# VectorE's low half of a weight one fetch after ScalarE's high half, in the attention part of block 1

## The reference, cut to what matters

```
for i in range(2):
    h = rms_norm(x, ln_attn_g[i])
    dq, dk, dv, mq, mk, mv = split(h @ w_in[i])        # six sections of 512 columns
    dq, dk, mq, mk = rms_norm(each head of them)
    y_diff = diff_attention(dq, dk, dv, ...)           # 4 heads, two score maps each
    y_moba = moba_attention(mq, mk, mv, ...)           # 8 heads; 256 tokens are one block
    x = x + concat(y_diff, y_moba) @ w_out[i]
    x = x + conv_ffn(rms_norm(x, ln_ffn_g[i]), ...)    # not touched
```

## Time and profile before

| | us |
|---|---|
| median of three timed runs (2045.48 to 2047.96) | 2046.79 |
| the profiled execution, its own time | 2051.6 |
| its span in the trace | 2049.8 |
| mean granted TensorE clock, share of full speed | 0.996 |

### The profile page before, as it was taken

How to read it: one execution, slowest core, us unless ns; L and a number is a source line. 1 busy time by engine, 2 the same in 40 slices (tenths; PEclk the granted TensorE clock), 3 DMA queues, 4 the chain that set the end, 5 groups by cost and what they waited for, 6 DMA issues and landing times.

```text
span 2049.8 us, 33452 instructions
## 1 busy us (share of the span) xinstructions
PE 2009.4 (98%) x13114; PEld 1738.3 (85%) x13114; DVE 1330.0 (65%) x2339; ACT 955.7 (47%) x1574; POOL 159.3 (8%) x169
## 2 busy tenths in 40 slices
PE   9999999999999999999999999999999999999998
PEld 7779998878999888888888788888878899888997
DVE  6767667767877337476445555868566686575665
ACT  4655555565555434353432453233246454445444
POOL 2001000000110100000200001111110000100100
PEclk9999999999999999999999999999999999999999
DMA  8446665535555322222222104534234244441554
GB/s 248 148 142 245 228 225 196 181 108 175 186 176 191 137 93 81 75 83 83 72 93 93 52 31 157 193 116 161 92 129 154 93 135 155 134 154 57 193 172 134
DMA packets 79706, 285.54 MB, mean 139 GB/s; under 512 B 8976, under 2 KB 9644, under 8 KB 79552
## 3 DMA queue, kind: packets, MB, share of 16 engines
q1 hardware_dynamic: 71136, 256.93, 37.7%
q10 hardware_dynamic: 6416, 19.51, 2.7%
q0 software_dynamic: 2000, 6.97, 1.3%
HBM read 277.55 MB, written 5.83 MB: 138 GB/s over the span
## 4 chain that ended last, share of the span: by engine, by line
PE 81%; DVE 10%; ACT 6%; issue 2%; DMA 1%; POOL 0%; ACTq 0%; DVEq 0%; SPq 0%
PE pb L1124 16%; PE pb L1126 15%; PE pb L1125 15%; PE pb L1137 6%; PE pb L1139 6%; PE pb L1138 6%; DVE SPL L2222 3%; ACT SPH L1637 3%; PE pb L1143 3%; PE pb L1302 2%; PE pb L1496 2%; PE pb L1303 2%; PE pb L1304 2%; PE pb L1477 2%; PE pb L1391 1%
## 5 line engine op out<-in xcount | busy, mean ns | idle before, releaser
L2222 DVE TENSOR_TENSOR SPL<-RAW,SPH 128x1024 fp32r<-128x1024 f32 x460 | 558.9, 1232 | 367.2 <-ACT SPH L1637 343.4
L1637 ACT ACTIVATE SPH<-RAW 128x1024 fp32r<-128x1024 f32 x462 | 477.4, 1052 | 208.4 <-PE pb L1126 111.3
L1124 PE MATMUL pb<-HTH,SPH 128*128 128x256 f32 (+1 forms) x1304 | 447.0, 343 | 8.4 <-POOL HTL L2881 3.1
L1126 PE MATMUL pb<-HTH,SPL 128*128 128x256 f32 (+1 forms) x1304 | 437.9, 336 | 0.0
L1125 PE MATMUL pb<-HTL,SPH 128*128 128x256 f32 (+1 forms) x1304 | 437.5, 335 | 0.0
L1124 PEld LDWEIGHTS pb<-HTH,SPH 128*128 128x128 f32 x1304 | 247.8, 190 | 36.8 <-ACT HTH L1686 3.2
L1126 PEld LDWEIGHTS pb<-HTH,SPL 128*128 128x128 f32 x1304 | 247.8, 190 | 26.1
L1125 PEld LDWEIGHTS pb<-HTL,SPH 128*128 128x128 f32 x1304 | 248.0, 190 | 24.8
L1137 PE MATMUL pb<-SPH,HTH 128*128 128x512 f32 x640 | 254.6, 398 | 2.1 <-DVE SPL L2222 1.4
L1139 PE MATMUL pb<-SPL,HTH 128*128 128x512 f32 x640 | 249.9, 390 | 0.0
L1138 PE MATMUL pb<-SPH,HTL 128*128 128x512 f32 x640 | 249.8, 390 | 0.0
(11 more groups left out here) (297 smaller groups left out, 2853.2 us busy)
## 6 DMA issues: line engine op xcount, KB each, us to landing
RAW<-in_w_up SPq DMA_DIRECT2D x88, 512.0 KB, 4.5
RAW<-in_wa SPq DMA_DIRECT2D x64, 512.0 KB, 3.5
RAW<-in_w_in SPq DMA_DIRECT2D x48, 512.0 KB, 4.7
RAW<-in_wmg SPq DMA_DIRECT2D x48, 512.0 KB, 3.5
RAW<-in_wbr SPq DMA_DIRECT2D x48, 512.0 KB, 3.5
RAW<-in_w_down SPq DMA_DIRECT2D x44, 512.0 KB, 4.9
RAW<-in_w_ada SPq DMA_DIRECT2D x24, 512.0 KB, 4.7
ARAW<-in_w_ada ACTq DMA_DIRECT2D x24, 512.0 KB, 4.2
```

The costliest lines, as they stand in the source:

```text
L1124: T.matmul(o, wh[:, kt, :], xh[:, kt, n0:n1], start=kt == 0, stop=False)
L1126: m = T.matmul(o, wl[:, kt, :], xh[:, kt, n0:n1], start=False, stop=kt == 7)
L1637: A.activation(hi, raw, ACT.Copy, scale=1.0).then_inc(*act.tick(s["hi"], ("u", u)))
L2222: W.tensor_tensor(lo, raw, hi.bitcast(F32), SUB).then_inc(*dve.tick(s["lo_dve"], ("u", u)))
```

## The change

VectorE's half of a split becomes a step of its own, split_low. ScalarE still does its half at the step split. split_upto notes each split weight in self.pending; lows adds split_low for all that are noted. Outside block 1's attention part, and wherever split_upto is called directly, lows follows at once. Inside it (self.later is True from the start of the sections until the heads and the output projection are done) get_w leaves the new ones pending and adds them at the next call of get_w, ahead of that call's own splits. A weight is never left pending at its own fetch.

```
@@ -151,6 +151,7 @@
         self.held, self.loaded, self.ready, self.off_raw = set(), set(), {}, set()
         self.slots, self.raw_before, self.slot_before = [None] * NS, {}, {}
         self.split_on, self.limit = [0], 1 << 30
+        self.later, self.pending = False, []
         self.run()
 
     def add(self, *step):
@@ -182,16 +183,21 @@
             self.loaded.add(u)
             self.loads += 1
 
-    def split_upto(self, n):
+    def lows(self):
+        for u in self.pending:
+            self.add("split_low", u)
+        self.pending = []
+
+    def split_upto(self, n, later=False):
         while self.order is not None and self.splits <= n and self.splits < len(self.order):
             u = self.splits
             self.load_upto(u + NR - 1)
             if u not in self.loaded:
-                return
+                break
             if self.order[u][3] == "split":
                 q = self.nsplit % NS
                 if q in self.held:
-                    return
+                    break
                 self.held.add(q)
                 eng = "pool" if self.split_on[self.nsplit % len(self.split_on)] else "dve"
                 self.nsplit += 1
@@ -200,7 +206,10 @@
                 self.slots[q] = u
                 self.off_raw.add(u)
                 self.add("split", u)
+                self.pending.append(u)
             self.splits += 1
+        if not later:
+            self.lows()
 
     def get_w(self, name, idx, cols=1024, kind="split"):
         self.used.append((name, idx, cols, kind))
@@ -208,7 +217,10 @@
         self.gets += 1
         if self.order is not None:
             assert self.order[u] == (name, idx, cols, kind)
-            self.split_upto(min(u + NS + 1, self.limit))
+            self.lows()
+            self.split_upto(min(u + NS + 1, self.limit), self.later)
+            if u in self.pending:
+                self.lows()
         return u
 
     def put_w(self, u):
@@ -499,6 +511,7 @@
         if l:
             self.add("mark", f"qkv{l}")
         rows, heads = self.qkv(l, made), self.attn1(l, range(16))
+        self.later = True
         for n, _ in enumerate(rows):
             if n < 4 and l == 0:
                 next(turned)
@@ -528,6 +541,8 @@
                     else:
                         next(heads)
         drain(heads)
+        self.later = False
+        self.lows()
         made = self.norm_filled(f"f{l}", (7,), [(f"w_up{l}", i) for i in (0, FF_TILES, 1)])
         self.ada_ring = (3,)
         for t in range(2):
@@ -2796,7 +2811,7 @@
         W.tensor_tensor(x[:, 512:1024], x[:, 512:1024], sb["AFX"][:, t, 512:1024], ADD).then_inc(
             *dve.tick(o, ("x", l, t)))
 
-    does = {"start": start, "cs": cs, "lam": lam, "split": split, "ada_turn": ada_turn, "adv": adv, "adv_end": adv_end,
+    does = {"start": start, "cs": cs, "lam": lam, "split_low": split, "ada_turn": ada_turn, "adv": adv, "adv_end": adv_end,
             "adv_fin": adv_fin, "stats": stats, "scale": scale, "prod": prod, "bias_rows": bias_rows, "mask": mask, "picks": picks,
             "qk_scale": qk_scale, "qk_sums": qk_sums, "scores": scores,
             "probs": probs, "y": y, "y_turn": y_turn, "res1": res1, "up": up, "rope": rope, "res2": res2,
@@ -2943,7 +2958,7 @@
         G.dma_start(sb["AFX"][:, 0:n, :], k.args["xscr"][0, 0:n * 128, :].rearrange("(t p) d -> p t d", p=128)
                     ).then_inc(*pool.tick(s["x_back"]))
 
-    does = {"start": start, "qk_turn": qk_turn, "split": split, "bias_rows": bias_rows, "consts": consts, "ctx_in": ctx_in,
+    does = {"start": start, "qk_turn": qk_turn, "split_low": split, "bias_rows": bias_rows, "consts": consts, "ctx_in": ctx_in,
             "bias_back": bias_back, "prod": prod, "up": up, "keep": keep, "gnorm": gnorm,
             "split_a": split_a, "split_z": split_z, "branch": branch, "x_back": x_back}
     for step, *a in sched.steps:
```

## The result

| | median, us | runs | ratio to before | 95% interval |
|---|---|---|---|---|
| before, beside it | 2045.26 | 2044.27 to 2047.96 | | |
| the changed kernel | 2051.72 | 2049.67 to 2052.88 | 1.0028 | 1.0018 to 1.0037 |
| the changed kernel, second timing | 2051.25 | 2049.21 to 2054.06 | 1.0024 | 1.0015 to 1.0033 |

So the change costs 5.7 us (3.7 to 7.6) by the first timing and 4.9 us (3.1 to 6.8) by the second. The forecast was +5.6 us, 2052.4 us. The profiled execution took 2051.72 us.

The account below looks back on a forecast made before the run. TensorE, busy 98%, bounds it, so VectorE's order counts only through TensorE's idle time. 6.05 + 2.2 - 3.9 - 1.0 + 0.6 + 1.6 = +5.6 us on the median 2046.8 gives 2052.4 us, range 2048.5 to 2057.0.

Parts of the forecast that it names:

- Part 1: Layer 0's first section: TensorE waits for the late low half of weight 4 (numbered as fetched, from 0), loss 6.05 us.
- Part 2: Just after the wait at weight 4: TensorE's clock falls to half, loss 2.2 us, between 1.4 and 3.0.
- Part 3: Layer 0's heads: low halves stop holding up score steps, TensorE's waits of 1.64, 1.26, 0.98 go, gain 3.9 us.
- Part 4: Layer 1's heads: TensorE's wait of 0.98 us at 437.69 goes, gain 1.0 us, ends 0 and 3.05.
- 5, weight 124: Layer 1's first section: weight 124's low half moves behind qk_scale, ending 366.76; TensorE had started it at 366.15, loss 0.6 us.
- Part 6: End of both output projections: one more low half delays the norm's statistics, loss 0.8 us a layer, 1.6 in all.
- Rival "absorbed": Before layer 0's heads: arrival of weights 12 to 14 sets their start, TensorE's loss costs nothing; -2.7 us, chance 0.07.
- part 3's gain stays away: Layer 0's heads: ScalarE is the slower, TensorE's waits stay; up to +10.5, 2056.5 us with half gone, chance 0.13.
- Loads slip: Layer 0's first sections: loads of weights 9, 10, 11 slip behind TensorE, up to 4 us, 2056 us, chance 0.10.
- The signs to look for: Trace: TensorE idle 6 us from 25.7, clock 0.5, no RR wait over 1 us, VectorE's under 8, norms under 1 late.

Follow-up runs that it names:

- burst at once: The changed kernel, but layer 0's low halves of weights 4, 5 and 6 made at once as before; 2044.84 us, ratio 0.9989.
- 7 fillers: The kernel before, with layer 0's low halves 4, 5 and 6 late and 7 filler matmuls ahead of weight 4; 2052.30 us, ratio 1.0028.
- only the burst late: The kernel before, with only layer 0's low halves of weights 4, 5 and 6 behind section 0's scaling; 2052.41 us, ratio 1.0029.
- layer 1 only: The kernel before, with low halves late only in layer 1, from the first score maps and not at the end; 2043.72 us, ratio 0.9986.
- from weight 7, not the end: The changed kernel, but low halves 4 to 6, 124 and the last two ahead of each norm made at once; 2041.12 us, ratio 0.9973.
- end at once: The changed kernel, but the last two low halves of each output projection made at once as before; 2048.57 us, ratio 1.0004.
- only 6 late: The kernel before, with only layer 0's low half of weight 6 late, behind section 0's scaling; 2046.09 us, ratio 1.0004.

## Why the prediction came out right, point by point

| part | forecast | in the trace of the changed kernel | who shows it |
|---|---|---|---|
| 1 and 2, weight 4 and the clock | +8.25 | +8.74 (6.2 and 2.5) | burst at once; 7 fillers |
| 3, layer 0's heads | -3.9 | -4.85 | only the burst late |
| 4, layer 1's heads | -1.0 | -2.11 | layer 1 only |
| 5, weight 124 | +0.6 | +0.85 | from weight 7, not the end |
| 6, two norms | +1.6 | +0.78 and +0.66 | end at once |
| sum | +5.6 | +4.1 (at 506: +3.9) | timed: +5.7 and +4.9 |

That the forecast meets the first timing to 0.1 us is luck in part: the interval is 4 us wide, parts 3 and 4 are each off by about 1 us, and parts 3 and 6 have a cause beside the one that I gave.

- **Part 1** is right in place, size and releaser: 6.02 us idle. The trick was to look for a twin of the chain that nothing had disturbed, in layer 1.
- **Part 2** is right: the clock falls, and it is worth 2.5 us against 2.2. The Trainium skill, "TensorE: Matmul & The Clock Gate", part 1, says "the ramp penalty is <1% of a typical kernel span; don't fit to a specific cold count". The rows agree with the size (2.5 of 2050 us is 0.1%), but in a question of 0.2% it is about a quarter of all the losses (2.5 of 11.0 us), so here it had to be counted.
- **Part 3** is right in size by accident of two things. Each wait is worth more than its idle figure: the waits of 1.64, 1.26 and 0.98 us moved TensorE by 1.83, 1.42 and 1.15 (the columns have 1.85, 1.57 and 1.44, with some of 0.1 to 0.2 between them), since a matmul is shown with 0.39 us and the next could have started after 0.23. And its cause was incomplete. I took all of it for VectorE's queue. With only the burst late 2.9 of the 4.85 us come back without the lag, because the chain of the maps started when the loads let it and TensorE had been early for it. What the lag adds on top of the late start is 2.0 us; without a late start it is the whole, less the 1.5 us that belonged to one execution: some 3.4 us. The forecast of 3.9 had these 1.5 us in it too, since it was read from the same trace.
- **Rival "absorbed"** is the one that I dismissed with the wrong argument. I wrote that TensorE "has not one idle gap in that stretch", and that this spoke against slack. The slack lay further on, in the very waits on RR that I had booked as part 3's gain. They could be taken back once, not twice. In the changed kernel both reasons act and the sum comes out the same, so the error didn't show in the number. It would have in each half alone: 8.4 expected for the burst, 5.9 measured. The price of the other rival, that part 3's gain stays away, was also wrong: with half of parts 3 and 4 gone the sum is +8.1, 2054.9 us, not 2056.5.
- **Part 4** is the term that was mis-sized. I counted the one wait of 0.98 us; in all kernels with the lag TensorE gains 1.15 there and 0.3 and 0.5 us at two waits near 410 and 422 us, which I had set to nothing because they are shown with 0.15 and 0.24 us.
- **Part 6** is right with 0.8 and 0.7. But the pair of residual rows ends at 141.30 by the earlier trace rows and not at 141.0; by that the statistics would have come some 1.0 us later, and what they came later is 0.7, so the sum had the better figure by luck. And that the later ada weight costs filler time only is wrong in layer 0: it brought a wait of 1.3 us on its load, and TensorE's own work behind that wait ended last, by some 0.1 us, beside the late statistics. In one of two profiles the clock fell after it.
- **Loads slip** was seen only in small, in the runs with 7 fillers and with only 6 late (0.9 and 1.0 us at 46).
- **The signs to look for** all came: the 6 us on SPL, PEclk 0.50, no wait over 1 us on RR in the heads, 21.2 us down to 5.7, the norms late by under 1 us.
- **The median.** I set the forecast on the median of three runs and added the parts, though the profiled execution lay 4.8 us above. This was right: what it had more is not the change's. One piece is the 1.5 us of loads; others come behind 1500 us, where the changed kernel's profile catches up 4.3 us on that of before, and that of layer 1 only, whose work there is the same as before's, 4.2 us. One stretch at half clock in before, which those two lack, is 1.7 us of it:

```profile
1832.00:1835.20 3.20, 3.20 (x16) 3.20 (x16) 0.00 (x0) 0.44 (x2) 0.00 (x0) 0.50 0.95 353
```

What stays open: whether the changed kernel costs 3.9 or 5.7 us. The traces' sums (+3.9 and +4.7 at 506 us) and the two timings are within each other's intervals, and end at once has 2.45 in the trace and 0.8 (-0.8 to 2.7) timed. The execution of before that all rows of the table share explains part of it: in 12 of the 13 timings the cost lies above the column at 506, by 0.8 us in the mean of all, and its late loads in layer 0 are worth up to 1.5.

## What to carry to other kernels

A queued step with slack should be moved behind its neighbours only where the neighbour is what somebody waits for: here the same rule was worth -7 us beside the score maps of both layers and +6 us in one burst ahead of a section, and one number (from which fetch it holds) decides the sign. Two waits in one stretch may be one slack seen twice, so take each cause away alone before adding gains and losses. And measure a move by the starts of the same matmuls in both traces rather than by idle figures or spans: these place every loss and gain of a trace to about 0.1 us where the timing knows 2 us. They don't average over executions, though: take a second profile of the kernel before, since one execution can differ from another by 1.5 us in its loads.

## What was not expected of the hardware

- Filler matmuls on fp32 data that isn't split (one column of ones, read 512 times) take 0.87 us for 512 columns and are shown as two records; the kernel's own 512-column matmuls start 0.23 us apart. No run tells whether the data type or the way of reading does it.
- A wait of 3.3 us brought the clock to 1.2 GHz shortly after the restart (full pace up to 32.9 us, half from there), a wait of 6 us before it. Waits of 0.7 to 1.6 us in the same section and beside the heads did not, but of the six waits of 1.19 to 1.37 us on the ada load at the norms, among small matmuls (in both profiles of the changed kernel and in burst at once), one, of 1.37 us, did (0.51 from 149.4 to 152.6 us).
- The same loads in the same order landed up to 1.5 us apart between two executions, with the DMA engines busy 0.94 of the time from 20 to 52 us in both, and this moved TensorE by as much, 13 us later.
